# Moving the rounding of the last weight piece of each slot from GpSimd to ScalarE

## The chip, the cores and the metric

The kernel runs on one core of a Trainium2 chip. The metric is device time in microseconds, the median of several executions. An experiment on a changed kernel is compared with runs of the kernel before on the same chip.

## The reference

The reference is a two-layer decoder trunk over 256 tokens of width 1024. Each layer does RMSNorm, four mixer branches behind gates, cross-attention over 256 memory tokens, and a mixture of 16 experts. Only the last part matters here:

```
# hier_moe: top group, top 2 experts in it, weights `combine`
for e in range(16):
    he = silu(h @ w_gate[e]) * (h @ w_up[e])        # 1024 -> 512
    out = out + combine[..., e:e+1] * (he @ w_down[e])   # 512 -> 1024
```

All is float32. Each expert has three weight matrices of 2 MB (gate, up, down), and all 16 experts of both layers are loaded: 32 x 6 MB.

## The kernel before, in words

Before the expert stage of a layer runs the mixing, the cross-attention and the router; the change touches none of their instructions. In the expert stage the kernel goes through the 16 experts in order. One run through one expert is called a turn. The matrices land in three slots of the tile `ring`, one each for gate, up and down, and SyncE (SP) issues one load a slot as soon as the slot is free (L384 to L396).

TensorE multiplies in the float32r format, so each float32 weight is used as a sum of two float32r parts: `w_hi`, the rounded weight, and `w_lo`, the difference between the weight and `w_hi`. A slot is cut into four pieces of 128 x 1024, so an expert has twelve pieces, numbered n = 4j + i, where j = 0, 1, 2 is gate, up, down and i = 0 to 3 is the piece in the slot. `w_hi` and `w_lo` have six buffers (RP = 6): piece n may be written once TensorE has used piece n - 6, which the semaphore `w_used` tells.

For pieces i = 0, 1, 2 (`SHARED_PIECES`), ScalarE rounds (`pieces`, L1198, a Copy recorded at L994) and VectorE subtracts (`pieces`, L1858, recorded at L1863). For piece i = 3, GpSimd does both (`piece`, L1440: a cast at L1448, then a subtraction at L1451). The order of the work is written out by hand; every engine runs its own list in order and waits on semaphores. For one turn it is:

- TensorE (L910): gate product from pieces 0 to 3 ("widen 0"), transposed picks (L920), up product from pieces 4 to 7 ("widen 1"), then what fills the time until the activation is there: gathers for the next group of four experts (L871) and the scatter of the expert before (L885, L886), transposes of `hid` (L937), down product from pieces 8 to 11 (L948, L949).
- ScalarE (L1213): pieces 4, 5, 6, copy of the gate product (`gl`), `pickT`, piece 8, Silu, copy of the up product (`ul`), one gather copy (`ga`, not in the last four turns), pieces 9 and 10, copy of the transposed `hid` (`hidT`), pieces 0, 1, 2 of the next expert, two copies `y_hi`.
- VectorE (L1943): subtractions for 4, 5, 6, `gl` sum (L1947), subtraction for 8, `ul` sum (L1950), `hid` (L1954), subtraction for 9, gather copy `ga` (L1940), `hidT` low part (L1960), subtraction for 10, subtractions for 0, 1, 2 of the next expert, two `y_lo` (L1968).
- GpSimd (L1454): piece 7, copy of `pickT` to the upper partitions (L1460), piece 11, piece 3 of the next expert.

A slot is free for the next load when both VectorE's three subtractions (`w_lo`) and GpSimd's one (`w_lo_p`) from it are done.

Of the kernel before, what the change touches and what calls it, by code (L numbers as in the profile page):

```python
# [30 lines left out]
N_EXP = 16  # L31
# [39 lines left out]
def split_piece_used(n):  # L71
# [2 lines left out]

PER_TURN = dict(w_hi=9, w_lo=9, w_hi_p=3, w_lo_p=3, w_used=12, ga_mm=2, ga_ev_a=1, ga_ev_v=1,
                pickT_mm=1, pickT=1, pickT_p=1, gu_cp=2, gu_sum=2, act_gate=1, hid=1,
                hidT_mm=1, hidT_hi=1, hidT_lo=1, y_mm=1, y_hi=2, y_lo=2)
PER_PASS = dict(pick=1, sc_mm=4, x_acc=4)  # L80
# [2 lines left out]
RP = 6  # L83
# [5 lines left out]
SHARED_PIECES = (0, 1, 2)  # L89
# [7 lines left out]
def trunk(nc, T, out):  # L97
    with ExitStack() as ctx:  # L98
        def sb(name, shape, dt=F32):
            return ctx.enter_context(nc.sbuf_tensor(name, shape, dt))  # L100
# [3 lines left out]
        def sem(name):  # L104
            if name not in sems:
                sems[name] = ctx.enter_context(nc.semaphore(name))
            return sems[name]
# [154 lines left out]
        w_hi = sb("w_hi", [P, RP, PIECE], F32R)  # L262
        w_lo = sb("w_lo", [P, RP, PIECE], F32R)
# [40 lines left out]
        ld = [sem(f"loaded{s}") for s in range(NS)]  # L304
        slot_of = [i % NS for i in range(NCH)]
        e_slot = slot_of[ND:ND + 3]
        dense_loads = [slot_of[:ND].count(s) for s in range(NS)]
        loads = [n + PASSES * N_EXP for n in dense_loads]
# [27 lines left out]
        def turns_before(name, l, p, e):  # L336

            return (l * PASSES + p) * (N_EXP * PER_TURN[name]) + e * PER_TURN[name]

        def passes_before(name, l, p):  # L340

            return (l * PASSES + p) * PER_PASS[name]

        def skipped(name):

            return (PASSES - 1) * (N_EXP * PER_TURN[name] if name in PER_TURN else PER_PASS[name])

        def done_in_pass_0(name, l):

            return turns_before(name, l, 1, 0) if name in PER_TURN else passes_before(name, l, 1)  # L350

# [637 lines left out]
        def _(act):  # L989
            q = Order(act, "act")  # L990
            A = nc.scalar.activation

            def copy(dst, src, **kw):
                return A(dst, src, ACT.Copy, **kw)  # L994
# [37 lines left out]
            with act.Fori(0, L) as l:  # L1032
# [165 lines left out]
                def pieces(p, e, j, which):  # L1198

                    s_ = e_slot[j]  # L1200
                    act.wait_ge(ld[s_], l * (16 * loads[s_]) + 16 * (dense_loads[s_] + 1) + p * (16 * N_EXP) + e * 16)
                    for i in which:
                        n = 4 * j + i
                        act.wait_ge(sem("w_used"), turns_before("w_used", l, p, e) + n + 1)
                        copy(w_hi[:, n % RP, :], ring[:, s_, i * PIECE:i * PIECE + PIECE]).then_inc(sem("w_hi"), 1)

                def gathered(p, b, g, k):

                    act.wait_ge(sem("ga_mm"), turns_before("ga_mm", l, p, 0) + g * KD + k + 1)
                    copy(ga[:, g % 2, k].rearrange("p e a c -> p a e c"),  # L1210
                         bank[b][:].rearrange("p (a e c) -> p a e c", a=2, e=GROUP)).then_inc(sem("ga_ev_a"), 1)

                def turn(p, e):  # L1213
                    g, i = e // GROUP, e % GROUP
                    pieces(p, e, 1, SHARED_PIECES)

                    act.wait_ge(sem("w_used"), turns_before("w_used", l, p, e) + RP + 4)
                    copy(gl, bank[0][CAP:P, :]).then_inc(sem("gu_cp"), 1)
                    act.wait_ge(sem("pickT_mm"), turns_before("pickT_mm", l, p, e) + 1)
                    both = bank[2][0:CAP, 0:TB * IDC].rearrange("p (t n) -> p t n", t=TB)  # L1220
                    copy(pickT[0:CAP, e % 2, :].rearrange("p (t n) -> p t n", t=TB), both[:, :, 0:P])
                    copy(cw_parts[0:CAP], both[:, :, P + e:IDC:N_EXP], accum_out=cw[0:CAP, :]).then_inc(sem("pickT"), 1)
                    pieces(p, e, 2, (0,))
                    act.wait_ge(sem("gu_sum"), turns_before("gu_sum", l, p, e) + 1)
                    A(gl, gl, ACT.Silu).then_inc(sem("act_gate"), 1)

                    act.wait_ge(sem("w_used"), turns_before("w_used", l, p, e) + RP + 8)
                    copy(ul, bank[1][CAP:P, :]).then_inc(sem("gu_cp"), 1)
                    if g + 1 < GROUPS:
                        gathered(p, 0, g + 1, 2 * i)  # L1230
                    pieces(p, e, 2, (1, 2))
                    act.wait_ge(sem("hidT_mm"), turns_before("hidT_mm", l, p, e) + 1)
                    copy(hidT[:, :, 0, :], bank[1][:, 0:4 * CAP].rearrange("p (t c) -> p t c", t=4)).then_inc(sem("hidT_hi"), 1)
                    if e < N_EXP - 1:
                        pieces(p, e + 1, 0, SHARED_PIECES)
                    for nh in range(2):
                        if nh == 0:
                            act.wait_ge(sem("y_mm"), turns_before("y_mm", l, p, e) + 1)
                        else:

                            act.wait_ge(sem("w_used"), turns_before("w_used", l, p, e) + RP + 12)
                        copy(y_hi[:, nh * 512:nh * 512 + 512], bank[2 + nh][:]).then_inc(sem("y_hi"), 1)

                def one_pass(p):
                    if not isinstance(p, int):
                        pieces(p, 0, 0, SHARED_PIECES)
                    for k in range(0, KD, 2):
                        gathered(p, 4 + k % 4, 0, k)
                    for e in range(N_EXP):
                        turn(p, e)  # L1250

                pieces(0, 0, 0, SHARED_PIECES)
                for tb in range(TB):
                    act.wait_ge(sem("h_gained"), l * PER["h_gained"] + tb + 1)
                    copy(hs_hi[:, tb], h[:, tb, :].rearrange("p (f k) -> p k f", k=KD)).then_inc(sem("hs_hi"), 1)
# [1 line left out]
                A(rx[:, 2].rearrange("p a b -> p (a b)"), rx[:, 1].rearrange("p a b -> p (a b)"), ACT.Exp)  # L1257
                A(rx[:, 7].rearrange("p a b -> p (a b)"), rx[:, 6].rearrange("p a b -> p (a b)"), ACT.Exp).then_inc(sem("rt_x2"), 1)
                one_pass(0)

                act.wait_ge(sem("flag"), l + 1)
                more = q.more_passes()
                with act.If(more):
                    with act.Fori(1, PASSES) as p:
                        one_pass(p)
# [16 lines left out]
        def _(pool):  # L1282
            q = Order(pool, "pool")
            g = nc.gpsimd
# [63 lines left out]
            with pool.Fori(0, L) as l:  # L1348
# [66 lines left out]
                for n in range(16):  # L1415
                    i, tb, nh = n // 4, (n // 2) % 2, n % 2
                    pool.wait_ge(sem("mg_ev"), l * PER["mg_ev"] + n + 1)
                    q.settle()
                    src = gs[:, tb, i % 2, nh * 512:nh * 512 + 512]
# [20 lines left out]
                def piece(p, e, j):  # L1440
                    n = 4 * j + 3
                    s_ = e_slot[j]
                    pool.wait_ge(ld[s_], l * (16 * loads[s_]) + 16 * (dense_loads[s_] + 1) + p * (16 * N_EXP) + e * 16)
                    q.settle()
                    pool.wait_ge(sem("w_used"), turns_before("w_used", l, p, e) + n + 1)
                    q.settle()
                    src = ring[:, s_, 3 * PIECE:4 * PIECE]
                    g.tensor_copy(w_hi[:, n % RP, :], src).then_inc(sem("w_hi_p"), 1)  # L1448
                    pool.wait_ge(sem("w_hi_p"), turns_before("w_hi_p", l, p, e) + j + 1)
                    q.settle()  # L1450
                    g.tensor_tensor(w_lo[:, n % RP, :], src, w_hi[:, n % RP, :].bitcast(F32),  # L1451
                                    ALU.subtract).then_inc(sem("w_lo_p"), 1)

# [30 lines left out]
                        one_pass(p)  # L1484
                with pool.Else():

                    for name in ("w_hi_p", "pickT_p"):
                        pool.wait_ge(sem(name), done_in_pass_0(name, l))
                        pool.sem_inc(sem(name), skipped(name))
                    pool.wait_ge(sem("w_lo_p"), done_in_pass_0("w_lo_p", l) + LO_P_BIAS)  # L1490
                    pool.sem_inc(sem("w_lo_p"), skipped("w_lo_p"))
                q.leave()
# [7 lines left out]
        def _(dve):  # L1500
            q = Order(dve, "dve")
# [91 lines left out]
            with dve.Fori(0, L) as l:  # L1593
# [8 lines left out]
                s_ = lambda i: sp[:, i, :]  # L1602
# [65 lines left out]
                for n in range(8):  # L1668
# [4 lines left out]
                    for i in range(2):  # L1673
                        hd = n % 4 + 4 * i
                        src = rl[:, n % 2, i * wide:i * wide + wide]
# [30 lines left out]
                for u in range(3):  # L1706
                    dve.wait_ge(sem("dl_mm"), l * PER["dl_mm"] + u + 1)
                    n, wide = (4, P) if u == 0 else (2, S)
# [149 lines left out]
                def pieces(p, e, j, which):  # L1858

                    for i in which:  # L1860
                        n = 4 * j + i
                        dve.wait_ge(sem("w_hi"), turns_before("w_hi", l, p, e) + 3 * j + i + 1)
                        v.tensor_tensor(w_lo[:, n % RP, :], ring[:, e_slot[j], i * PIECE:i * PIECE + PIECE],  # L1863
                                        w_hi[:, n % RP, :].bitcast(F32), ALU.subtract).then_inc(sem("w_lo"), 1)

# [175 lines left out]
```

## Time and profile before

| what | value |
|---|---|
| median of 3 runs | 1618.54 us (1616.63 to 1620.39) |
| the profiled execution | 1624.06 us |
| its span | 1622.4 us |
| mean granted TensorE clock in it | 0.903 of full speed |
| busy: TensorE, VectorE, ScalarE, GpSimd | 1302.4, 977.4, 660.9, 753.3 us |

The profile is of one execution. A busy time is the union of an engine's instructions; an instruction that is held up after its start still counts as busy, so the duration of a single instruction is to be read beside the shortest of its kind. In the timeline, instructions of one kind that follow each other are merged into one line with their count ("x4") and the time from the first start to the last end. Times in brackets are idle time of the engine before the line, with what ended it.

### The profile page before, as it was taken

Reading aid. Unit: us, or ns where it says so; the run is one execution under the profiler, and the core shown is the slowest. Engines: PE = TensorE matmul, PEld = TensorE weight load, DVE = VectorE, ACT = ScalarE, POOL = GpSimd, SP = SyncE. Lnnn points to the kernel's source line nnn. Section 1 sums busy time; section 2 is a strip of 40 time slices with the busy share of each in tenths; the row PEclk is TensorE's granted clock in tenths of the full one; section 3 lists DMA queues with packets and bytes.
Section 4 is the critical chain, followed back from the end, with each engine's and each line's share of the span. In section 5 each row is a group of like instructions: output and inputs, shape, how many; then the busy total and the mean of one; then the engine's idle time right before and its main releaser. Section 6 shows DMA issues by size and latency. Waiting matters only on the chain. (4 is left out here: it accounts for less than half of the span.)

```text
span 1622.4 us, 18087 instructions
## 1 busy us (share of the span) xinstructions
PE 1302.4 (80%) x5124; PEld 934.1 (58%) x5124; DVE 977.4 (60%) x1261; ACT 660.9 (41%) x1005; POOL 753.3 (46%) x625
## 2 busy tenths in 40 slices
PE   4999978999487877787769998898975777777773
PEld 2874644676365655565548645466854565556552
DVE  3306365422679888888622254654127888898885
ACT  4122303322365655555430412043234655556552
POOL 5730063200656666776436202612007666766663
PEclk8999989999589999998879998999996889999987
DMA  8443213432557777878264431164144777877771
GB/s 218 132 156 104 104 52 120 152 143 104 124 209 267 275 292 272 302 281 292 103 203 131 156 105 52 52 217 146 52 169 70 266 273 290 298 278 281 289 287 60
DMA packets 58384, 299.25 MB, mean 184 GB/s; under 512 B 4016, under 2 KB 8224, under 8 KB 45728
## 3 DMA queue, kind: packets, MB, share of 16 engines
q1 hardware_dynamic: 55536, 294.07, 50.9%
q0 software_dynamic: 2736, 3.87, 2.2%
q8 instruction: 48, 0.79, 0.2%
q14 instruction: 64, 0.52, 0.1%
HBM read 296.88 MB, written 1.05 MB: 184 GB/s over the span
## 5 line engine op out<-in xcount | busy, mean ns | idle before, releaser
L1863 DVE TENSOR_TENSOR w_lo<-ring,w_hi 128x1024 fp32r<-128x1024 f32 x288 | 482.4, 1718 | 8.8 <-ACT w_hi L994 6.8
L994 ACT ACTIVATE w_hi<-ring 128x1024 fp32r<-128x1024 f32 x328 | 330.0, 1054 | 40.7 <-PE bank L533 26.4
L906 PE MATMUL bank<-w_hi,ga 128*128 128x512 f32 x512 | 226.1, 442 | 101.3 <-DVE w_lo L1863 83.9
L1448 POOL CAST w_hi<-ring 128x1024 fp32r<-128x1024 f32 x96 | 181.6, 1892 | 204.4 <-PE bank L949 170.9
L1451 POOL TENSOR_TENSOR w_lo<-ring,w_hi 128x1024 fp32r<-128x1024 f32 x96 | 267.7, 2789 | 17.9 <-POOL w_hi L1448 17.9
L468 PE MATMUL bank<-ring,hT 128*128 128x512 f32 (+2 forms) x576 | 217.9, 539 | 4.0 <-ACT hT L1029 2.2
L907 PE MATMUL bank<-w_lo,ga 128*128 128x512 f32 x512 | 215.3, 420 | 0.0
L906 PEld LDWEIGHTS bank<-w_hi,ga 128*128 128x128 f32 x512 | 104.4, 204 | 155.2 <-DVE w_lo L1863 109.9
L468 PEld LDWEIGHTS bank<-ring,hT 128*128 128x128 f32 x576 | 113.5, 199 | 102.0 <-issue 96.7
L948 PE MATMUL bank<-w_hi,hidT 128*128 128x512 f32 x256 | 120.1, 469 | 41.7 <-DVE hidT L1960 41.7
L462 PE MATMUL bank<-hT,ring 128*128 128x256 f32 (+1 forms) x544 | 119.3, 380 | 1.9 <-DVE hT L1569 1.9
L949 PE MATMUL bank<-w_lo,hidT 128*128 128x512 f32 x256 | 116.4, 455 | 0.0
L907 PEld LDWEIGHTS bank<-w_lo,ga 128*128 128x128 f32 x512 | 105.4, 206 | 19.0
L462 PEld LDWEIGHTS bank<-hT,ring 128*128 128x128 f32 (+1 forms) x544 | 99.9, 184 | 20.7 <-DVE hT L1569 2.3
L948 PEld LDWEIGHTS bank<-w_hi,hidT 128*128 128x128 f32 x256 | 58.2, 227 | 59.1 <-issue 37.9
L1408 POOL TENSOR_TENSOR gk<-dl,E 128x512 f32<-128x512 f32 x8 | 10.1, 1267 | 170.8 <-DVE dl L1777 170.8
L1804 DVE TENSOR_TENSOR w_lo<-ring,w_hi 128x1024 fp32r<-128x1024 f32 x40 | 49.4, 1275 | 63.8 <-ACT w_hi L994 63.8
L1426 POOL TENSOR_TENSOR h<-h,gs 128x512 f32<-128x512 f32 x24 | 33.8, 1433 | 104.3 <-DVE gs L1785 104.3
L1287 POOL DMA_DIRECT2D gul<-in_norm_ffn x2 | 1.3, 635 | 172.2 <-DVE x L1851 172.2
L994 ACT ACTIVATE gul<-bank 64x512 f32<-64x512 f32 x64 | 38.1, 595 | 82.8 <-PE bank L907 82.7
L531 PE MATMUL bank<-w_hi,hT_hi 128*128 128x512 f32 x160 | 64.6, 404 | 3.9 <-DVE hT_lo L1821 3.9
L1072 ACT ACTIVATE gs<-bank 128x512 f32<-128x512 f32 x32 | 19.1, 597 | 116.6 <-PE bank L468 93.9
(441 smaller groups left out, 2151.9 us busy)
## 6 DMA issues: line engine op xcount, KB each, us to landing
ring<-in_w_e_gate SPq DMA_DIRECT2D x32, 2048.0 KB, 8.1
ring<-in_w_e_up SPq DMA_DIRECT2D x32, 2048.0 KB, 8.2
ring<-in_w_e_down SPq DMA_DIRECT2D x32, 2048.0 KB, 8.1
ring<-in_w_in SPq DMA_DIRECT2D x24, 2048.0 KB, 8.3
ring<-in_w_ckv SPq DMA_DIRECT2D x4, 2048.0 KB, 9.6
ring<-in_w_branch SPq DMA_DIRECT2D x4, 2048.0 KB, 10.3
ring<-in_w_out SPq DMA_DIRECT2D x4, 2048.0 KB, 11.2
ring<-in_w_cq SPq DMA_DIRECT2D x2, 2048.0 KB, 14.7
```

What stands on the lines that cost most here:

```text
L462: ins = mm(dst, w[:, k, c0:c0 + m], src[:, k, :], start=(k == 0), stop=(k == KD - 1))
L468: ins = mm(dst, src[:, k, tb * P:tb * P + P], w[:, k, c0:c1], start=(k == 0), stop=(k == KD - 1))
L531: mm(bank[b0 + tb][:], t_hi, w_hi[:, n % RP, c], start=(k == 0), stop=False)
L906: mm(bank[j][:], tile, w_hi[:, n % RP, c], start=(k == 0), stop=False)
L907: ins = mm(bank[j][:], tile, w_lo[:, n % RP, c], start=False, stop=(k == KD - 1))
L948: mm(bank[2 + nh][:], tile, w_hi[:, n % RP, c], start=(t == 0), stop=False)
L949: ins = mm(bank[2 + nh][:], tile, w_lo[:, n % RP, c], start=False, stop=(t == 3))
L994: return A(dst, src, ACT.Copy, **kw)
L1448: g.tensor_copy(w_hi[:, n % RP, :], src).then_inc(sem("w_hi_p"), 1)
L1451: g.tensor_tensor(w_lo[:, n % RP, :], src, w_hi[:, n % RP, :].bitcast(F32), ALU.subtract).then_inc(sem("w_lo_p"), 1)
L1804: v.tensor_tensor(w_lo[:, n % RP, :], ring[:, s_, i * PIECE:i * PIECE + PIECE], w_hi[:, n % RP, :].bitcast(F32), ALU.subtract).then_inc(se ...
L1863: v.tensor_tensor(w_lo[:, n % RP, :], ring[:, e_slot[j], i * PIECE:i * PIECE + PIECE], w_hi[:, n % RP, :].bitcast(F32), ALU.subtract).then ...
```

## The change

ScalarE rounds all four pieces of every slot, GpSimd only subtracts for piece 3, and it waits for ScalarE's semaphore `w_hi` in place of its own waits for the load and for `w_used`. ScalarE's copies go at the end of each group of pieces: piece 7 before the `gl` copy, piece 11 before the `hidT` copy, piece 3 of the next expert before the `y_hi` copies, and in the router stage piece 3 of the first expert before the copies of `h`. The counts of `w_hi` follow.

```diff
-PER_TURN = dict(w_hi=9, w_lo=9, w_hi_p=3, w_lo_p=3, w_used=12, ga_mm=2, ga_ev_a=1, ga_ev_v=1,
+PER_TURN = dict(w_hi=12, w_lo=9, w_lo_p=3, w_used=12, ga_mm=2, ga_ev_a=1, ga_ev_v=1,
@@ ScalarE, turn
-                    pieces(p, e, 1, SHARED_PIECES)
+                    pieces(p, e, 1, range(4))
@@
-                    pieces(p, e, 2, (1, 2))
+                    pieces(p, e, 2, (1, 2, 3))
                     act.wait_ge(sem("hidT_mm"), turns_before("hidT_mm", l, p, e) + 1)
                     copy(hidT[:, :, 0, :], ...).then_inc(sem("hidT_hi"), 1)
                     if e < N_EXP - 1:
-                        pieces(p, e + 1, 0, SHARED_PIECES)
+                        pieces(p, e + 1, 0, range(4))
@@ ScalarE, router stage
-                pieces(0, 0, 0, SHARED_PIECES)
+                pieces(0, 0, 0, range(4))
@@ GpSimd, piece
-                    pool.wait_ge(ld[s_], l * (16 * loads[s_]) + 16 * (dense_loads[s_] + 1) + p * (16 * N_EXP) + e * 16)
-                    q.settle()
-                    pool.wait_ge(sem("w_used"), turns_before("w_used", l, p, e) + n + 1)
+                    pool.wait_ge(sem("w_hi"), turns_before("w_hi", l, p, e) + n + 1)
                     q.settle()
                     src = ring[:, s_, 3 * PIECE:4 * PIECE]
-                    g.tensor_copy(w_hi[:, n % RP, :], src).then_inc(sem("w_hi_p"), 1)
-                    pool.wait_ge(sem("w_hi_p"), turns_before("w_hi_p", l, p, e) + j + 1)
-                    q.settle()
                     g.tensor_tensor(w_lo[:, n % RP, :], src, w_hi[:, n % RP, :].bitcast(F32),
                                     ALU.subtract).then_inc(sem("w_lo_p"), 1)
@@ VectorE, pieces
-                        dve.wait_ge(sem("w_hi"), turns_before("w_hi", l, p, e) + 3 * j + i + 1)
+                        dve.wait_ge(sem("w_hi"), turns_before("w_hi", l, p, e) + n + 1)
```

## Rows read from the trace of the kernel before

**Rows 1.** The page: busy time of each engine; a load's median time to landing.

```profile
PE 1302.4 (80%) x5124; PEld 934.1 (58%) x5124; DVE 977.4 (60%) x1261; ACT 660.9 (41%) x1005; POOL 753.3 (46%) x625
...
ring<-in_w_e_down SPq DMA_DIRECT2D x32, 2048.0 KB, 8.1
```

**Rows 2.** The `ul` sums of the first expert stage: durations, first and last start.

```profile
L1950 DVE TENSOR_TENSOR gul<-bank,gul x16: 682/683/684, 459.8 to 795.4; 64x512 f32<-64x512 f32 x16
```

**Rows 3.** Windows: length; busy PE, PEld, DVE, ACT, POOL (instructions); granted clock, DMA share, GB/s.

```profile
459.80:795.40 335.60, 259.03 (x1017) 197.41 (x1018) 290.20 (x238) 193.72 (x283) 228.13 (x107) 0.90 0.76 275
...
592.90:594.90 2.00, 2.00 (x9) 1.65 (x10) 1.67 (x2) 0.63 (x1) 1.52 (x2) 1.00 0.96 270
...
615.10:618.80 3.70, 3.67 (x10) 2.96 (x11) 1.70 (x2) 0.63 (x1) 3.04 (x3) 0.54 0.88 275
```

**Rows 4.** Waits in 459.8 to 795.4: total us, times, longest.

```profile
POOL w_hi L1448 <- PE bank L949: 86.0, 15, 6.5
PEld bank L906 <- DVE w_lo L1863: 55.0, 30, 2.6
```

**Rows 5.** Timeline of VectorE, from one `ul` sum to the second one after it.

```profile
575.11 0.68 DVE L1950 TENSOR_TENSOR gul<-bank,gul 64x512 f32<-64x512 f32 x1 [2.65 <-ACT gul L994]
...
576.68 1.23 DVE L1863 TENSOR_TENSOR w_lo<-ring,w_hi 128x1024 fp32r<-128x1024 f32 x1
...
578.43 0.41 DVE L1960 TENSOR_TENSOR hidT<-bank,hidT 128x256 fp32r<-128x256 f32 x1
578.76 5.46 DVE L1863 TENSOR_TENSOR w_lo<-ring,w_hi 128x1024 fp32r<-128x1024 f32 x4
584.15 1.27 DVE L1968 TENSOR_TENSOR y_lo<-bank,y_hi 128x512 fp32r<-128x512 f32 x2
585.35 7.50 DVE L1863 TENSOR_TENSOR w_lo<-ring,w_hi 128x1024 fp32r<-128x1024 f32 x3
592.77 0.68 DVE L1947 TENSOR_TENSOR gul<-bank,gul 64x512 f32<-64x512 f32 x1
...
595.68 0.68 DVE L1950 TENSOR_TENSOR gul<-bank,gul 64x512 f32<-64x512 f32 x1 [1.11 <-ACT gul L994]
596.55 2.05 DVE L1954 SCALAR_TENSOR_TENSOR gul<-gul,cw 64x512 f32<-64x512 f32 x1 [0.19 <-DVE gul L1950]
...
615.00 0.67 DVE L1947 TENSOR_TENSOR gul<-bank,gul 64x512 f32<-64x512 f32 x1
...
619.47 0.68 DVE L1950 TENSOR_TENSOR gul<-bank,gul 64x512 f32<-64x512 f32 x1 [2.67 <-ACT gul L994]
```

**Rows 6.** Timeline of VectorE, single subtractions out of the merged lines.

```profile
582.16 2.06 DVE L1863 TENSOR_TENSOR w_lo<-ring,w_hi 128x1024 fp32r<-128x1024 f32 x1
...
589.46 3.39 DVE L1863 TENSOR_TENSOR w_lo<-ring,w_hi 128x1024 fp32r<-128x1024 f32 x1
```

**Rows 7.** Timeline of GpSimd in the same turn.

```profile
581.25 1.89 POOL L1448 CAST w_hi<-ring 128x1024 fp32r<-128x1024 f32 x1 [5.33 <-PE bank L949]
583.32 3.15 POOL L1451 TENSOR_TENSOR w_lo<-ring,w_hi 128x1024 fp32r<-128x1024 f32 x1 [0.18 <-POOL w_hi L1448]
...
588.63 3.13 POOL L1451 TENSOR_TENSOR w_lo<-ring,w_hi 128x1024 fp32r<-128x1024 f32 x1 [0.18 <-POOL w_hi L1448]
...
595.66 2.40 POOL L1451 TENSOR_TENSOR w_lo<-ring,w_hi 128x1024 fp32r<-128x1024 f32 x1 [0.18 <-POOL w_hi L1448]
```

**Rows 8.** Timeline of ScalarE in the same turn.

```profile
575.60 1.99 ACT L994 ACTIVATE w_hi<-ring 128x1024 fp32r<-128x1024 f32 x2
577.89 0.38 ACT L994 ACTIVATE hidT<-bank 128x256 fp32r<-128x256 f32 x1 [0.30 <-PE bank L937]
...
582.48 1.09 ACT L994 ACTIVATE y_hi<-bank 128x512 fp32r<-128x512 f32 x2 [1.22 <-PE bank L949]
...
588.80 1.05 ACT L994 ACTIVATE w_hi<-ring 128x1024 fp32r<-128x1024 f32 x1
```

**Rows 9.** Timeline of SyncE: the load of the next `down` matrix.

```profile
580.26 0.33 SPq L396 DMA_DIRECT2D ring<-in_w_e_down  x1
```

More of the change, by code:

```diff
@@ L1245, in one_pass @@
                     if not isinstance(p, int):
-                        pieces(p, 0, 0, SHARED_PIECES)
+                        pieces(p, 0, 0, range(4))
                     for k in range(0, KD, 2):
@@ L1485, in _ @@
                 with pool.Else():
-                    for name in ("w_hi_p", "pickT_p"):
-                        pool.wait_ge(sem(name), done_in_pass_0(name, l))
-                        pool.sem_inc(sem(name), skipped(name))
+                    pool.wait_ge(sem("pickT_p"), done_in_pass_0("pickT_p", l))
+                    pool.sem_inc(sem("pickT_p"), skipped("pickT_p"))
                     pool.wait_ge(sem("w_lo_p"), done_in_pass_0("w_lo_p", l) + LO_P_BIAS)
```

## The prediction, made before the changed kernel was run

> **What bounds the kernel now.** I read the busy times first. TensorE is busy for 80% of the span and VectorE for 60% [rows 1], but the change touches only the two expert stages. The window over the first of them, from the first `ul` sum at 459.8 us to the last at 795.4 [rows 2], says more: 15 turns in 335.6 us, 22.37 us a turn, VectorE busy for 290.2 of it (86%), TensorE 259.0, GpSimd 228.1, ScalarE 193.7, DMA share 0.76 [rows 3]. The waits come next: TensorE waits 30 times for VectorE's `w_lo`, 55.0 us in total, while GpSimd sits idle for 86.0 us before its cast of piece 3, waiting for TensorE to use piece 9 [rows 4]. So the loop is closed by VectorE, and GpSimd has time to spare.
>
> Then the timeline of VectorE over two turns [rows 5]. Their periods, from `ul` sum to `ul` sum, are 595.68 - 575.11 = 20.57 and 619.47 - 595.68 = 23.79 us; I call them short and long. I read this pair as the steady pattern; it makes 44.36 us, 22.18 a turn. In the short turn VectorE has no idle time of note from `hidT` at 578.43 to the `gl` sum at 592.77, so each microsecond lost in that stretch moves the turn. Behind the `gl` sum lie TensorE's last two up pieces, the `ul` copy and the `ul` sum: 2.91 us in the short turn and 4.47 in the other. The difference is the clock: 1.00, the 2.4 GHz level, in 592.9 to 594.9, but 0.54, most of it at 1.2 GHz, in 615.1 to 618.8 [rows 3]; in the second case TensorE had just stood still for want of the same `w_lo`. The mean tail is 3.69.
>
> **What holds VectorE.** A subtraction alone takes 1.23 us at 576.68 [rows 5]. The one at 582.16 takes 2.06 and the one at 589.46 takes 3.39 [rows 6]. Beside GpSimd's rows this has one reading. The cast runs 581.25 to 583.14; the subtraction started at 582.16 ends 1.08 us after the cast does. GpSimd's subtraction issued at 588.63 ends at 591.76; the VectorE one issued at 589.46 ends at 592.85, again 1.09 later [rows 6, 7]. GpSimd's own takes 2.40 when nothing is in its way (595.66) and 3.15 when it is issued inside a VectorE subtraction [rows 7]. So a VectorE operation on two SBUF tensors and a GpSimd subtraction exclude each other, and a GpSimd one that is waiting goes before VectorE's next. A full hit costs VectorE 3.39 - 1.23 = 2.16 us, a cast 2.06 - 1.23 = 0.83. `y_lo`, with one operand in PSUM, runs 1.27 for two beside GpSimd's 3.15 and pays nothing [rows 5, 7]. `hid` does pay: 2.05 us at 596.55 under the subtraction of 595.66 [rows 5, 7].
>
> The page "SBUF — State Buffer" of the Trainium skill (section on the two separate sides) says in my words that whoever starts first holds the shared ports for its whole instruction and the other is fully blocked. The trace agrees for the subtractions and not for the cast: the cast of 581.25 started while VectorE was inside a subtraction, and neither was lengthened. What the rule as stated would make of the sum is the third rival.
>
> **The change, part by part (short turn, zero at the `ul` sum, 575.11).**
>
> 1. Removed: three casts a turn on GpSimd. Two of them hit VectorE. The line of three (585.35, 7.50 us) is 3 x 1.13 us of issue distance (5.46 for four, less one 0.83 hit, gives 1.13 to 1.16) plus 4.0 of blocking: 2.16 for the full subtraction, 0.83 for a cast, and about 1.0 for the tail of the subtraction of 583.32, which runs to 586.47 [rows 5 to 7]. The line of four contains the other 0.83. The third cast lies in VectorE's idle time. Gain: 2 x 0.83 = 1.7 us. Bounds: 0, if something else ends those waits, and 2 x 1.89, a cast's whole duration.
>
> 2. Added: three ScalarE copies of 1.0 us (1.99 for two [rows 8]).
>  - Piece 7: ScalarE's idle 1.2 us before `y_hi`, and VectorE's lateness in the up pieces, cover it. The `gl` copy after it is not wanted before the `gl` sum. Cost 0, and 1.0 without that cover.
>  - Piece 11, before `hidT`: ScalarE ended its two copies at 577.59 and was idle for 0.30 until TensorE's transposes were there [rows 8]. The third copy ends at about 578.6, so `hidT`, the `hidT` low part and the start of the down product come 0.7 us later. Cost 0.7 (bounds 0 and 1.0). In the last four turns ScalarE has no `ga` copy ahead, and I take 0.2.
>  - Piece 3 of the next expert needs piece 9 used, 581.25 before. ScalarE has 1.22 us idle before `y_hi` [rows 8], and the copy fits. Cost 0 (bound 1.0).
>
> 3. Moved: the GpSimd subtractions, and this decides.
>  - Piece 11. Before, the subtraction ran at 573.54, in VectorE's wait for `ul`, or at 595.66, where it held `hid`. Now it starts when ScalarE's third copy ends: 1.99 + 0.49 + 1.0 + 0.18 (the handover on GpSimd [rows 7]) = +3.65, and runs to +6.05. VectorE issues the subtraction for piece 10 at 578.76 + 0.7, +4.35, and is held to +6.05, so it ends at +7.1 in place of +5.55. Cost 1.55; bounds 0 (it falls in idle time) and 2.16.
>  - Piece 3 of the next expert. ScalarE's copy ends at about +7.75 and GpSimd asks at +7.9, in the middle of VectorE's four. Before it was at +8.2 but met the two `y_lo`, so only 1.0 was lost. Now `y_lo` is 2.2 us further away, and the hit is full: 2.16 - 1.0 = 1.15. Bounds -1.0 and 1.15.
>  - Piece 7. Its copy is the fourth after `y_hi` and waits for piece 1 to be used; GpSimd asks near the end of `y_lo` and hits one of the three up subtractions, as before. Cost 0; bounds -2.16 and 0.
>
> 4. Semaphores. The wait for `w_used` and for the load leave GpSimd; ScalarE makes both before it rounds, so nothing is queued behind them that was not. A GpSimd wait now holds `pickT_p` behind piece 7; TensorE's scatter wants that only after the next up product. 0.
>
> 5. Loads. The `down` slot is freed at +7.1 and not at 580.26, +5.15 [rows 9]. With 8.1 us to landing [rows 1] it is there at +15.2. ScalarE rounds piece 8 at 588.80, +13.7 before and over 15 after, ahead of a Silu that waits for the `gl` sum. Hidden; without that cover up to 1.5. The other two have more room.
>
> The sum for a turn with gathers: 0.7 - 1.7 + 1.55 + 1.15 = +1.7 us at the `gl` sum, which stood at 592.77 - 575.11 = +17.66 and goes to about +19.4. In the long turn the `gl` sum stood at 615.00 - 595.68 = +19.32: it had paid a held `hid` (1.3) and a slow down product. Both of these vanish in VectorE's backlog afterwards: `hid` meets no subtraction any more, and `y_hi`, at +8.8 with the fast clock and at most +11 with the slow one, is ready before VectorE ends its four at +12.7. So after the change every turn is like the long one up to the `gl` sum: 19.4. I leave the tail as it is, 3.69 on average. Then a turn is 23.1 against 22.18: +0.92.
>
> Thirty turn intervals make 27.6. The measured mean, 22.37, exceeds the pair's 22.18 by 0.19, which is 5.7 us over 30: those other turns are slower already, and I take half of it as absorbing part of the cost, -2.8. The last turn of each stage also holds a delayed down product, 0.5 each, +1. In the router stage GpSimd loses a cast ahead of its subtraction, but VectorE's queue there is held by what follows it as well: 0, within 2 a layer. Sum +26. The profiled execution, 1624.06 us (span 1622.4), would become 1650; it stood 5.5 us above the median, so the median goes from 1618.5 to about 1645.
>
> **Rivals.**
> - Faster. The two cast hits vanish and the subtractions cost no more than today. One mechanism: which VectorE operation a GpSimd subtraction meets. For: GpSimd becomes idle by 5.7 us a turn, and VectorE is the bound. Against: subtraction 11 starts at +3.65 and the low part of `hidT` at +4.0, so the VectorE burst is right behind it. It decides if that subtraction and that of piece 3 still meet `ul`, `ga` or `y_lo`. Price: 1.7 in the short turn, 0.83 in the long one, 1.27 x 30 = 38: 1580; with ScalarE's 0.7 in 24 turns charged, 1597.
> - Only ScalarE's delay counts: 0.7 x 24 = 17: 1636. For: VectorE's blocking might merely change places. Against: the sum above.
> - The exclusive hold as the page states it. Each cast hit is then worth 1.89, not 0.83, and point 1 gains 2.1 more a short turn: 0.92 - 1.05 on average, so about 1615, no change. Against: the 2.06 row [rows 6].
> - The clock. TensorE stands still for longer after the change. If every tail ran at 1.2 GHz (4.47 in place of 3.69), 0.78 x 30 = 23 more: 1668. If every tail were fast, 1622.
>
> **How the numbers follow.** My forecast, with the subtraction hits and a mixed clock (1636 to 1655), has 0.50; only ScalarE's delay or fast tails (1622 to 1636) 0.12; slow tails (1655 to 1672) 0.12; no change 0.08; faster 0.18. A measurement of this kernel tells 0.2%, 3.2 us, from no change. So slower 0.74, same 0.08, faster 0.18. Range 1604 to 1666: it leaves out most of the faster case and the end of the slow-clock case. The likeliest case's own range is 1622 to 1666.
>
> **What would show it.** In the trace after: `hidT` on ScalarE right behind a line of three roundings, with no idle time; GpSimd's subtraction about 3.6 us after the `ul` sum; in VectorE's line after `hidT` two held subtractions, so that four take over 8 us and not 5.46; the `gl` sum at 19.4 in nearly every turn, the alternation of 20.6 and 23.8 gone; no 2.06 us durations left. It is wrong if VectorE's durations of over 3 us are no more frequent than one or two a turn, if `y_lo` waits for `y_hi`, or if turns come out under 22.

## The result: slower by 2.1%, and where the time went

The changed kernel takes 1651.7 us (median of 4 runs, 1648.71 to 1656.16) against 1618.06 us for the kernel before (4 runs). The ratio is 1.0209, 95% interval 1.0182 to 1.0236. The forecast was 1645, and slower. The interval leaves no doubt that it is slower; whether by more or by less than 2% it does not settle. The profiled execution has a span of 1649.2 us, 26.8 more than the 1622.4 before. The profiled execution of the kernel before took 1624.06 us, 3.7 more than the longest of its four timed runs, while that of the changed kernel, 1650.97 us, lies at the median; so the spans differ by less than the medians.

First the page of the changed kernel, busy times and the largest group (line, engine, operation, shapes, count, then busy us and mean ns, then idle time before and what ended it):

```profile
PE 1316.2 (80%) x5124; PEld 925.2 (56%) x5124; DVE 1008.1 (61%) x1261; ACT 750.7 (46%) x1101; POOL 571.7 (35%) x529
...
L1857 DVE TENSOR_TENSOR w_lo<-ring,w_hi 128x1024 fp32r<-128x1024 f32 x288 | 536.0, 1903 | 8.7 <-ACT w_hi L994 7.9
```

GpSimd is busy for 181.6 us less than in [rows 1], and VectorE for 30.7 us more with the same 1261 instructions. Its added time is time in which its instructions are held up after their start. The numbers of three lines move: L1857 is L1863 of before, L1944 the `ul` sum L1950, L1941 the `gl` sum L1947, and GpSimd's subtraction is L1446.

The first expert stage, from the first `ul` sum to the last, by a window (length; busy PE, PEld, VectorE, ScalarE, GpSimd; granted clock, DMA share, GB/s), and the longest waits in it:

```profile
457.20:809.10 351.90, 272.41 (x1018) 196.98 (x1019) 308.01 (x238) 235.89 (x328) 140.38 (x60) 0.89 0.71 262
```

```profile
POOL w_lo L1446 <- ACT w_hi L994: 202.5, 45, 9.0
PEld bank L906 <- DVE w_lo L1857: 70.6, 64, 2.6
```

15 turns take 351.9 us, where [rows 3] had 335.6: 23.46 us a turn and not 22.37. GpSimd waits for ScalarE for 202.5 us, and the wait of TensorE's weight loads (PEld) for `w_lo` has grown from 55.0 [rows 4] to 70.6 us. So GpSimd was relieved and the engine that closes the loop was not.

One turn of VectorE, to be laid beside [rows 5]:

```profile
573.35 0.68 DVE L1944 TENSOR_TENSOR gul<-bank,gul 64x512 f32<-64x512 f32 x1 [2.52 <-ACT gul L994]
...
577.09 0.42 DVE L1954 TENSOR_TENSOR hidT<-bank,hidT 128x256 fp32r<-128x256 f32 x1 [0.34 <-ACT hidT L994]
577.43 8.62 DVE L1857 TENSOR_TENSOR w_lo<-ring,w_hi 128x1024 fp32r<-128x1024 f32 x4
585.97 1.28 DVE L1962 TENSOR_TENSOR y_lo<-bank,y_hi 128x512 fp32r<-128x512 f32 x2
587.16 5.86 DVE L1857 TENSOR_TENSOR w_lo<-ring,w_hi 128x1024 fp32r<-128x1024 f32 x3
592.95 0.67 DVE L1941 TENSOR_TENSOR gul<-bank,gul 64x512 f32<-64x512 f32 x1
...
597.25 0.68 DVE L1944 TENSOR_TENSOR gul<-bank,gul 64x512 f32<-64x512 f32 x1 [2.50 <-ACT gul L994]
```

The four subtractions after `hidT` take 8.62 us, before 5.46; the three up ones take 5.86, before 7.50. The `gl` sum stands at 592.95 - 573.35 = +19.60 us and the next `ul` sum at +23.90. Nearly every turn with gathers looks like this to three tenths, in both stages: the `gl` sum stands at +19.6 to +19.8, the next `ul` sum 4.1 to 4.4 us behind it, and the alternation of 20.57 and 23.79 is gone. Single subtractions out of these lines, and GpSimd's three, show the holds:

```profile
577.43 3.00 DVE L1857 TENSOR_TENSOR w_lo<-ring,w_hi 128x1024 fp32r<-128x1024 f32 x1
...
582.62 3.42 DVE L1857 TENSOR_TENSOR w_lo<-ring,w_hi 128x1024 fp32r<-128x1024 f32 x1
...
588.30 3.39 DVE L1857 TENSOR_TENSOR w_lo<-ring,w_hi 128x1024 fp32r<-128x1024 f32 x1
```

```profile
576.96 2.39 POOL L1446 TENSOR_TENSOR w_lo<-ring,w_hi 128x1024 fp32r<-128x1024 f32 x1 [8.93 <-ACT w_hi L994]
581.48 3.48 POOL L1446 TENSOR_TENSOR w_lo<-ring,w_hi 128x1024 fp32r<-128x1024 f32 x1 [2.13 <-ACT w_hi L994]
588.14 2.47 POOL L1446 TENSOR_TENSOR w_lo<-ring,w_hi 128x1024 fp32r<-128x1024 f32 x1 [3.18 <-ACT w_hi L994]
```

Each GpSimd subtraction now falls into a row of VectorE subtractions and costs it 1.8 to 2.2 us; the durations of 2.06 us, the cast hits of [rows 6], are gone. ScalarE shows why the first comes so late and with it `hidT`; there is no idle time before `hidT` now, where [rows 8] had 0.30:

```profile
573.84 2.94 ACT L994 ACTIVATE w_hi<-ring 128x1024 fp32r<-128x1024 f32 x3
576.68 0.37 ACT L994 ACTIVATE hidT<-bank 128x256 fp32r<-128x256 f32 x1
```

**The account.** I add up, turn by turn, the time from a `ul` sum to the `gl` sum and from there to the next `ul` sum (the tail), 30 turns in both stages. The first grows by 10.3 + 12.6 = 22.9 us, the tail by 6.0 + 5.7 = 11.7 us, together 34.6. Outside this, 7.7 us are won: 1.9 before anything that differs (at the start of the program), the rest in the router stages and behind the last `ul` sums. 34.6 - 7.7 is the 26.8 us of the spans, to rounding. Inside these sums, the first turn of each stage became shorter, 20.25 us and not 24.26. Why is not shown: with the same list of work on GpSimd, warm5_after below has 22.5 us there.

### The profile page after: what moved, and what is told of

It reads as the page before. It is cut to its first block and busy times, and to the rows that moved or that the text cites. A ratio compares the mean times of both kernels' runs of the same rounds, so it can differ in the third digit from the quotient of the medians.

```text
span 1649.2 us, 17857 instructions
## 1 busy us (share of the span) xinstructions
PE 1316.2 (80%) x5124; PEld 925.2 (56%) x5124; DVE 1008.1 (61%) x1261; ACT 750.7 (46%) x1101; POOL 571.7 (35%) x529
## 5 line engine op out<-in xcount | busy, mean ns | idle before, releaser
L1857 DVE TENSOR_TENSOR w_lo<-ring,w_hi 128x1024 fp32r<-128x1024 f32 x288 | 536.0, 1903 | 8.7 <-ACT w_hi L994 7.9
L994 ACT ACTIVATE w_hi<-ring 128x1024 fp32r<-128x1024 f32 x424 | 422.5, 1053 | 33.6 <-PE bank L533 24.8
L1446 POOL TENSOR_TENSOR w_lo<-ring,w_hi 128x1024 fp32r<-128x1024 f32 x96 | 266.5, 2776 | 445.9 <-ACT w_hi L994 445.9
L906 PE MATMUL bank<-w_hi,ga 128*128 128x512 f32 x512 | 237.1, 463 | 102.6 <-DVE w_lo L1857 93.9
L907 PE MATMUL bank<-w_lo,ga 128*128 128x512 f32 x512 | 222.2, 434 | 0.0
L907 PEld LDWEIGHTS bank<-w_lo,ga 128*128 128x128 f32 x512 | 109.3, 213 | 19.8
L949 PE MATMUL bank<-w_lo,hidT 128*128 128x512 f32 x256 | 110.6, 432 | 0.0
L948 PEld LDWEIGHTS bank<-w_hi,hidT 128*128 128x128 f32 x256 | 53.5, 209 | 93.5 <-issue 51.6
L1798 DVE TENSOR_TENSOR w_lo<-ring,w_hi 128x1024 fp32r<-128x1024 f32 x40 | 49.4, 1275 | 62.1 <-ACT w_hi L994 62.1
L1944 DVE TENSOR_TENSOR gul<-bank,gul 64x512 f32<-64x512 f32 x32 | 21.8, 682 | 70.3 <-ACT gul L994 70.3
L532 PE MATMUL bank<-w_lo,hT_hi 128*128 128x512 f32 x160 | 62.9, 393 | 0.0
## 6 DMA issues: line engine op xcount, KB each, us to landing
ring<-in_w_branch SPq DMA_DIRECT2D x4, 2048.0 KB, 10.3
```

Of the source, the lines that this page charges most:

```text
L532: mm(bank[b0 + tb][:], t_hi, w_lo[:, n % RP, c], start=False, stop=False)
L906: mm(bank[j][:], tile, w_hi[:, n % RP, c], start=(k == 0), stop=False)
L907: ins = mm(bank[j][:], tile, w_lo[:, n % RP, c], start=False, stop=(k == KD - 1))
L948: mm(bank[2 + nh][:], tile, w_hi[:, n % RP, c], start=(t == 0), stop=False)
L949: ins = mm(bank[2 + nh][:], tile, w_lo[:, n % RP, c], start=False, stop=(t == 3))
L1798: v.tensor_tensor(w_lo[:, n % RP, :], ring[:, s_, i * PIECE:i * PIECE + PIECE], w_hi[:, n % RP, :].bitcast(F32), ALU.subtract).then_inc(se ...
```

## The experiments

All ratios are to runs of the kernel before on the same chip. Theory A says that what counts is the place of each GpSimd operation in VectorE's line; B, that ScalarE's added work is the cost; C, TensorE's clock. "Turn by turn" means the two sums of the account above, each over 30 turns of the profiled execution. Line numbers differ from run to run; tile names and shapes tell what an instruction is.

### One slot at a time

ScalarE rounds the last piece of one slot only, and GpSimd keeps its cast for the other two:

```diff
-                    pieces(p, e, 1, SHARED_PIECES)          # up_only
+                    pieces(p, e, 1, range(4))
-                        pieces(p, e + 1, 0, SHARED_PIECES)  # gate_only
+                        pieces(p, e + 1, 0, range(4))
-                    pieces(p, e, 2, (1, 2))                 # down_only
+                    pieces(p, e, 2, (1, 2, 3))
```

> Of the change, only the up slot is done: ScalarE rounds piece 7, GpSimd keeps its casts of pieces 3 and 11. Theory A (exclusive hold between GpSimd and VectorE's two-input operations, and where each GpSimd operation falls): one cast hit of 0.83 us a turn goes and no subtraction moves into a worse place, so 0.8 x 30 = 24 us faster than before, about 1594. Theory B (the extra ScalarE work on the path is what costs): ScalarE has 1.2 us idle there, so within 3 us of before or slower. Theory C (only TensorE's clock): no ordered change.

Measured: 1590.25 us, ratio 0.983 (0.981 to 0.9849).

> Only the gate slot is done: ScalarE rounds piece 3 of the next expert. Theory A: the cast hit inside VectorE's line of four goes (0.83 in the short turn), the subtraction still meets y_lo and then one subtraction, 0.6 to 0.85 us a turn, so 18 to 25 us faster, about 1597. Theory B: same or slower, since the copy stands ahead of y_hi.

Measured: 1593.24 us, ratio 0.985 (0.982 to 0.988).

> Only the down slot is done: ScalarE rounds piece 11 before the hidT copy. Theory A: the whole loss sits here. hidT 0.4 us later, GpSimd's subtraction at +3.6 us holds the subtraction for piece 10 (1.8 us), y_lo moves away so that the subtraction of piece 3 hits in full (1.2 more) while a cast hit may go (0.8 less): the gl sum at about +20.2, turns of 24.3 us, 60 us slower than before, about 1678, so slower than the full change. Theory B: 0.4 us in 24 turns, about 10 us slower, 1628.

Measured: 1664.78 us, ratio 1.0295 (1.0276 to 1.0315).

The mean duration of a VectorE subtraction in the window 457 to 800 us goes the same way. One row each from up_only, gate_only and down_only (1706 ns before and 1896 ns after the whole change, in their first stage):

```profile
L1870 DVE TENSOR_TENSOR w_lo<-ring,w_hi 128x1024 fp32r<-128x1024 f32 x137 | 214.8, 1610 | 6.6 <-ACT w_hi L997 5.1
```

```profile
L1870 DVE TENSOR_TENSOR w_lo<-ring,w_hi 128x1024 fp32r<-128x1024 f32 x137 | 219.7, 1647 | 1.1 <-ACT w_hi L997 0.6
```

```profile
L1870 DVE TENSOR_TENSOR w_lo<-ring,w_hi 128x1024 fp32r<-128x1024 f32 x129 | 253.1, 2004 | 0.4 <-ACT w_hi L997 0.2
```

Two thirds of the change are each a gain of 1.5 to 1.7%, and the down slot alone loses 3%. The loss is less than the 60 us that were expected; the `gl` sum stands at about +20.5 there, but the tail is 3.53 us on average. The sum of the parts, -28 - 25 + 46 = -7 us, is not the whole, +34. Turn by turn, up_only and gate_only shorten the stretch up to the `gl` sum by 33 us each; on top of the down slot the two together shorten it by 31. The tails grow by 4 and 13 us in the single ones, and by 19 when both are put on top of the down slot. So what the casts of pieces 3 and 7 cost depends on where the rest stands, and a part of what is won before the `gl` sum is paid back in the tail. B does not explain two gains from added ScalarE work.

### ScalarE made slower, all else as before

```diff
-                        copy(w_hi[:, n % RP, :], ring[...]).then_inc(sem("w_hi"), 1)
+                        if i == 2:   # eight copies of 128 columns, the last one signals
+                            ...
```

> The kernel before, with ScalarE alone made slower: its rounding of the third piece of each slot is done in eight parts of 128 columns, which adds about 1 us where the change adds a whole rounding. GpSimd keeps its casts and subtractions. Theory A (place of the GpSimd holds): only the part before hidT is felt, 0.4 to 0.7 us in the 24 turns with gathers, so 0 to 17 us slower than before, 1618 to 1636. Theory B (ScalarE's added work makes the loss): 30 us or more slower, 1650.

Measured: 1619.5 us, ratio 1.0007 (0.9997 to 1.0017). The eight parts added less than meant: two roundings take 2.64 us, 0.65 more than in [rows 8], and the low part of `hidT` comes at 578.74 - 575.31 = +3.43, only 0.11 later than before.

```profile
575.80 2.64 ACT L994 ACTIVATE w_hi<-ring 128x1024 fp32r<-128x1024 f32 x9
578.35 0.36 ACT L994 ACTIVATE hidT<-bank 128x256 fp32r<-128x256 f32 x1
```

It shows that 0.65 us more of ScalarE work in each slot costs nothing that can be measured; for the full rounding ahead of `hidT` it is too weak a test.

### Piece 11 rounded behind hidT

```diff
-                    pieces(p, e, 2, (1, 2, 3))
+                    pieces(p, e, 2, (1, 2))
                     ...
                     copy(hidT[:, :, 0, :], ...).then_inc(sem("hidT_hi"), 1)
+                    pieces(p, e, 2, (3,))
```

> The changed kernel with ScalarE's rounding of piece 11 put behind the hidT copy. Theory A: hidT comes 0.4 us earlier, but GpSimd then asks inside VectorE's subtraction for piece 10 and the next one is held in full (2.2 in place of 1.8): the gl sum stays at +19.6 within 0.2, 1652 within 6. Theory B (ScalarE's delay of hidT): 0.4 to 0.7 us in 24 turns back, 10 to 17 us faster than the change, 1635 to 1642.

Measured: 1626.35 us, ratio 1.0053 (1.0036 to 1.007). That is 25 us faster than the change and outside both expectations, nearer to B's number than to A's. The trace shows that B's reason is not the one:

```profile
594.58 0.68 DVE L1945 TENSOR_TENSOR gul<-bank,gul 64x512 f32<-64x512 f32 x1 [1.10 <-ACT gul L994]
...
598.23 1.22 DVE L1858 TENSOR_TENSOR w_lo<-ring,w_hi 128x1024 fp32r<-128x1024 f32 x1
599.67 7.58 DVE L1858 TENSOR_TENSOR w_lo<-ring,w_hi 128x1024 fp32r<-128x1024 f32 x3 [0.23 <-ACT w_hi L994]
...
614.17 0.67 DVE L1942 TENSOR_TENSOR gul<-bank,gul 64x512 f32<-64x512 f32 x1
...
617.07 0.68 DVE L1945 TENSOR_TENSOR gul<-bank,gul 64x512 f32<-64x512 f32 x1 [1.10 <-ACT gul L994]
```

The low part of `hidT` is 0.43 us earlier and the subtraction for piece 10 runs freely, but the next ones are held in its place, and the `gl` sum is at 614.17 - 594.58 = +19.59, as A said, not a tenth better. What fell is the tail: 2.90 us for 4.30; turn by turn the tails are 30.6 us shorter and the stretches up to the `gl` sum 4.4 us longer. The stretch of the tail ran at full clock, that of the changed kernel (591.75 to 594.90) at 0.66:

```profile
614.20:616.40 2.20, 2.10 (x10) 1.77 (x11) 1.77 (x3) 0.63 (x1) 0.00 (x0) 1.00 0.78 164
```

```profile
591.75:594.90 3.15, 3.08 (x8) 2.16 (x9) 3.00 (x3) 0.63 (x1) 0.19 (x1) 0.66 0.89 281
```

The slow stretch is not gone, it lies earlier, behind another wait of TensorE: the granted clock is 0.55 from 607.2 to 611.0. There it does not delay the `gl` sum. Why it moved was not tested.

### TensorE kept busy in its idle time

Matmuls that serve nothing, into PSUM bank 3, which is free there:

```diff
+                def idle_work(p, e, count):
+                    if e > 0:
+                        pe.wait_ge(sem("y_lo"), turns_before("y_lo", l, p, e - 1) + 2)
+                    for _ in range(count):
+                        mm(bank[3][:, 0:256], hs_hi[:, 0, 0, :], pick[:, 0, 0:GROUP, :]..., start=True, stop=True)
@@ widen, ahead of each piece
+                        if n == 6:
+                            idle_work(p, e, 16)
@@ behind the transposes of hid
+                    idle_work(p, e, 10)
```

> The changed kernel with matmuls that serve nothing put into two idle times of TensorE: 16 of 256 columns ahead of piece 6, 10 behind the transposes of hid, into a PSUM bank that is free then. If the tail from the gl sum to the ul sum (4.3 us after, 2.9 with the fast clock) is long because TensorE has stood still before it, the tail falls to about 2.9 to 3.2 us and the time by 1.1 to 1.4 us in 30 turns, 33 to 42 us, to about 1613; the gl sum stays at +19.6. If the clock does not depend on that, the time is that of the change, 1652, or a little more.

Measured: 1679.14 us, ratio 1.0373 (1.0355 to 1.039), 27 us slower than the change. The clock did stay up (1.00 over the turn from 650.74 to 674.74), but I had put the work on the path. TensorE's timeline: piece 5 could start only at 669.14, and the sixteen matmuls then stood for 2.06 us ahead of piece 6, which was ready at about the time they began.

```profile
669.94 0.40 PE L917 MATMUL bank<-w_lo,ga 128*128 128x512 f32 x1
670.17 2.06 PE L903 MATMUL bank<-pick,hT_hi 128*128 128x256 f32 x16
672.07 0.40 PE L916 MATMUL bank<-w_hi,ga 128*128 128x512 f32 x1
```

With 14 of them ahead of piece 5 instead, in TensorE's wait itself, and 10 behind the transposes as in warm_after:

> The changed kernel with the same idle matmuls, but 14 of them ahead of piece 5, where TensorE waits 2.1 us for a held subtraction (in the run before they stood ahead of piece 6 and took 2.0 us on the path), and 10 behind the transposes. Theory: the clock stays at 2.4 GHz, the tail is 2.9 us and not 4.3, the gl sum stays at +19.6: 22.5 us a turn and 1.4 x 27 = 38 us faster than the change, 1612 to 1620. If the clock is not what makes the tail long: 1652 as the change.

Measured: 1624.81 us, ratio 1.0033 (1.0019 to 1.0047), 27 us faster than the change and 5 above the expected range. The window of the first stage shows a full clock, and the sums of one turn a tail of 618.32 - 615.41 = 2.91 us with the `gl` sum at +19.64:

```profile
457.20:800.00 342.80, 294.09 (x1408) 224.16 (x1407) 314.40 (x241) 240.72 (x334) 141.53 (x62) 1.00 0.73 270
```

```profile
595.77 0.68 DVE L1955 TENSOR_TENSOR gul<-bank,gul 64x512 f32<-64x512 f32 x1 [1.10 <-ACT gul L1005]
...
615.41 0.67 DVE L1952 TENSOR_TENSOR gul<-bank,gul 64x512 f32<-64x512 f32 x1
...
618.32 0.68 DVE L1955 TENSOR_TENSOR gul<-bank,gul 64x512 f32<-64x512 f32 x1 [1.10 <-ACT gul L1005]
```

Turn by turn the tails are 37.6 us shorter than in the changed kernel. The stretches up to the `gl` sum are 6.7 us longer, which comes from the first turn of each stage (19.6 us for 16.0), and 5.5 us more lie outside the turns; why is open. So most of the loss of 34 us depends on the clock in the tail. Does the same help the kernel before (14 ahead of piece 6, where that kernel waits, and 6 behind the transposes)?

> The kernel before with idle matmuls: 14 of 256 columns ahead of piece 6, where TensorE waits 2.1 us, and 6 behind the transposes. It tells what the clock alone costs before the change. In the long turn the slow clock costs 1.6 us in the tail and up to 1.8 in the down product; but after a fast tail GpSimd's subtraction for piece 11 meets hid (1.3 us), which a slow tail avoids. With a fast clock in every turn I expect turns of 21.4 to 22.2 us, 0 to 25 us faster than before, about 1605. Then the holds alone make the changed kernel with warm TensorE (1625) some 20 us slower. If it is at 1570 or less (every turn 20.6), the holds make 50 us and the clock took most of the gap away; if it is 1618, the clock costs the kernel before nothing.

Measured: 1617.08 us, ratio 0.9997 (0.9988 to 1.0007). No. A turn of it:

```profile
636.68 0.68 DVE L1961 TENSOR_TENSOR gul<-bank,gul 64x512 f32<-64x512 f32 x1 [1.11 <-ACT gul L1005]
637.55 2.06 DVE L1965 SCALAR_TENSOR_TENSOR gul<-gul,cw 64x512 f32<-64x512 f32 x1 [0.19 <-DVE gul L1961]
...
656.00 0.67 DVE L1958 TENSOR_TENSOR gul<-bank,gul 64x512 f32<-64x512 f32 x1
...
658.91 0.68 DVE L1961 TENSOR_TENSOR gul<-bank,gul 64x512 f32<-64x512 f32 x1 [1.10 <-ACT gul L1005]
```

The tails are all fast, 2.91 us, but now every turn is a long one up to the `gl` sum (+19.32), because GpSimd's subtraction for piece 11 meets `hid` each time (2.06 us). A turn of 22.25 us is the mean of the old pair. With TensorE kept busy in both kernels, the change costs 1624.8 - 1617.1 = 8 us; the other 26 come with the clock, as far as the idle matmuls, which stand at different places in the two, do nothing else. In the kernel before, a slow tail paid for itself, in the changed one it does not.

### No GpSimd subtraction at all

All twelve subtractions go to VectorE, which gives it 3 x 1.14 us more work a turn:

```diff
-                    pieces(p, e, 1, SHARED_PIECES)      # VectorE, likewise gate and down
+                    pieces(p, e, 1, range(4))
-                    piece(p, e, 1)                      # GpSimd, likewise the other two
```

> The change with GpSimd's subtraction taken away too: VectorE subtracts all twelve pieces. It adds 3 x 1.13 us of work to the engine that closes the loop and takes away three holds of 1.8, 2.2 and 2.2 us. Theory A: the gl sum comes at 19.6 - 6.2 + 3.4 = +16.8 us, turns of 19 to 20.5 us, 50 to 95 us faster than the changed kernel, 1560 to 1600, if loads keep up. Theory B (ScalarE): no better than the change, 1652, as ScalarE does the same. Plain work count on VectorE: 3.4 us a turn slower, 1750.

Measured: 1507.38 us, ratio 0.9317 (0.9296 to 0.9338): 144 us faster than the change and 111 faster than the kernel before. That is also 53 us below the lower end of what was expected. The engine with the longest line was given more to do and the turn fell from 23.9 to 18.62 us:

```profile
549.38 0.68 DVE L1913 TENSOR_TENSOR gul<-bank,gul 64x512 f32<-64x512 f32 x1 [0.19 <-ACT gul L984]
...
553.46 6.89 DVE L1826 TENSOR_TENSOR w_lo<-ring,w_hi 128x1024 fp32r<-128x1024 f32 x6
...
561.46 4.62 DVE L1826 TENSOR_TENSOR w_lo<-ring,w_hi 128x1024 fp32r<-128x1024 f32 x4
566.00 0.68 DVE L1910 TENSOR_TENSOR gul<-bank,gul 64x512 f32<-64x512 f32 x1
...
568.00 0.68 DVE L1913 TENSOR_TENSOR gul<-bank,gul 64x512 f32<-64x512 f32 x1 [0.19 <-ACT gul L984]
```

The `gl` sum is at +16.62 (expected +16.8). I had left the tail out of the gain: it is 2.00 us and not 2.9, since the `gl` sum now stands behind the subtraction for piece 7, so that one piece less is left for TensorE behind it. Turn by turn, 82.6 us are won up to the `gl` sum, where the holds were, and 65.0 us in the tails, where the shorter tail and the clock come together; this run does not separate those two. VectorE is busy for 96% of this stretch (159.81 of 166.60 us), with 341 GB/s of loads:

```profile
549.40:716.00 166.60, 147.82 (x614) 110.77 (x613) 159.81 (x169) 141.78 (x197) 18.97 (x9) 0.95 0.91 341
```

With the rounding of piece 11 put behind `hidT` as well:

> All twelve subtractions on VectorE, and ScalarE's rounding of piece 11 behind the hidT copy. With no GpSimd hold left, the 0.4 us of ScalarE before hidT should show undiluted: 0.4 x 24 = 10 us faster than the version with the rounding first, about 1497. If VectorE's own work fills the turn, less: 1507.

Measured: 1496.0 us, ratio 0.924 (0.9224 to 0.9255), 11 us faster than the version above. The low part of `hidT` comes at 552.00 - 548.69 = +3.31 and not +3.73, and with no hold left these 0.42 us of ScalarE show undiluted:

```profile
552.00 0.42 DVE L1924 TENSOR_TENSOR hidT<-bank,hidT 128x256 fp32r<-128x256 f32 x1
```

This is the best version found, 7.6% faster than the kernel before.

Last, GpSimd gets one subtraction back, for piece 7:

> As the version with all twelve subtractions on VectorE (1507), but GpSimd subtracts piece 7. The price of one hold by itself. Theory A: VectorE saves 1.13 us of its own and pays 2.16, 1.05 us a turn, 31 us in 30 turns: 1538. If GpSimd's help were help, 1.13 us a turn less: 1473.

Measured: 1535.95 us, ratio 0.9489 (0.9471 to 0.9507), 29 us slower than with none. The number is the expected one, the way there is not. The three up subtractions of VectorE run freely (3.49 us), and it is GpSimd's that is held, for 2.6 us of its 4.96:

```profile
568.64 3.49 DVE L1852 TENSOR_TENSOR w_lo<-ring,w_hi 128x1024 fp32r<-128x1024 f32 x3
572.04 0.67 DVE L1936 TENSOR_TENSOR gul<-bank,gul 64x512 f32<-64x512 f32 x1
572.64 2.80 DVE L1852 TENSOR_TENSOR w_lo<-ring,w_hi 128x1024 fp32r<-128x1024 f32 x1
```

```profile
569.40 4.96 POOL L1447 TENSOR_TENSOR w_lo<-ring,w_hi 128x1024 fp32r<-128x1024 f32 x1 [13.42 <-ACT w_hi L995]
```

It gets its turn only when the third has ended, and TensorE waits for piece 7 until 574.36. The turn has its `gl` sum at +15.5 us and a tail of 4.2, where the version with none has +16.6 and 2.0. Whoever is held, the piece costs more than the 1.14 us it saves.

## Why the prediction was right, and where it was not

- What bounds: right. VectorE's line closes the loop; without holds on it the stretch up to the `gl` sum fell from 19.6 to 16.62 us, with 3.4 us of work added (all_vector).
- Point 1, the casts: the price of 0.83 us a hit is right, the reading behind it is wrong. I took 1.89 us for a cast's own time and wrote that a cast started under a running subtraction lengthened neither and that the exclusive hold does not cover it. But a cast alone takes 1.04 us, as at 459.71, where VectorE has only the `ul` sum with its operand in PSUM, and in down_only at 568.69, beside `y_lo`:

```profile
459.71 1.04 POOL L1448 CAST w_hi<-ring 128x1024 fp32r<-128x1024 f32 x1 [0.49 <-POOL pickT L1460]
```

```profile
568.69 1.04 POOL L1455 CAST w_hi<-ring 128x1024 fp32r<-128x1024 f32 x1 [2.51 <-PE bank L910]
```

  The cast of 581.25 started under this subtraction, waited for its end at 582.25 and ended 0.89 us later; then the next VectorE subtraction, issued at 582.16, had its turn:

```profile
581.03 1.22 DVE L1863 TENSOR_TENSOR w_lo<-ring,w_hi 128x1024 fp32r<-128x1024 f32 x1
```

  Of the 94 casts from 457 us on in the kernel before, 2 take 1.04 us, and the other 92 end 0.89 to 0.91 us behind the end of a VectorE operation with two SBUF operands. So the exclusive hold is there for the cast as well, and with it a full hit costs 0.83 us. The third rival, which priced a hit at 1.89, had the right rule and the wrong price, and was no rival. Alone, the two slots bring 28 and 25 us, together 53, more than the 38 that the first rival allowed for all casts. A cast taken out also moves the subtraction behind it; how much of the rest that explains is not shown.
- Point 2, `hidT` later: 0.42 us measured (VectorE's low part at +3.74 against +3.32), 0.7 written. The time until GpSimd's subtraction, +3.61 for +3.65, was right. That the copies of pieces 3 and 7 cost nothing, as written, fits the gains of up_only and gate_only.
- Point 3, the moved subtractions: right in place and price. The durations of 3.00, 3.42 and 3.39 us are 1.77, 2.19 and 2.16 us of holding over 1.23; forecast were 1.55, 2.16 and 2.16. The `gl` sum was forecast at +19.4 in nearly every turn and stands at +19.6; the end of VectorE's four at +12.7 and at +12.7.
- The tail: wrong. I took the mean of one pair of turns, 3.69, and left it. Over all 30 turns it was 3.78 before and is 4.16 after (4.30 in the turn shown), which makes 11.7 us where I had written 0. The rival on the clock had 4.47, and warm5_after shows that it is the clock.
- Outside the turns: I wrote 0 for the router and +1 for the stage ends; they gave back 5.8 us, and 1.9 us more came before anything that differs. For the turns up to the `gl` sum I had 24.8 us after the absorbed part; they made 22.9: the first turns made 9.4 us less than before, and the other 28 made 1.15 us more each, where I had 0.92.
- The sum: in the profiled span +26 was forecast and +26.8 measured. That is partly luck, since 11.7 us of tail that I had not written met 7.7 us of gain that I had not written either. The median came out 6.7 us above 1645 in the last step, where I carried the 5.5 us between profiled execution and median over to the changed kernel: the profiled execution was forecast at 1650 and took 1650.97 us, which is 0.7 under the median and not 5.5 above it.
- The rule that a waiting GpSimd operation goes before VectorE's next one holds most of the time, not always. In the kernel before, 2 of the 94 casts waited for a further subtraction, this one up to 493.33; in vector_gp7 the subtraction waited for two further ones. What decides it stays open.

```profile
491.20 3.05 POOL L1448 CAST w_hi<-ring 128x1024 fp32r<-128x1024 f32 x1 [5.02 <-PE bank L949]
```

- What I did not see: that the kernel before has a second long way of 19.3 us which a fast clock brings out in every turn (warm_before), so that the holds alone, with TensorE kept busy in both, cost 8 us and not 26.

## What to carry to other kernels

Where two engines exclude each other, work given to the second is not free: its price is what it holds up on the first. Here a subtraction of 1.14 us on VectorE cost VectorE 2.2 us when GpSimd did it. Before relieving an engine that is not the bound, follow where its remaining operations will fall; one change made in three places can be two gains and one larger loss, so time the places apart. Read a duration beside the shortest of its kind before you call it the operation's own time: the cast's 1.89 us were 1.04 and a wait. And read the matmul rate behind every wait of TensorE: behind waits of the same 2.1 us the clock was full in one turn and low in the next.

## What the runs showed of the hardware

- A GpSimd subtraction of 128 x 1024 float32 from SBUF takes 2.39 us alone and a GpSimd cast of that size 1.04 us. Each excludes VectorE operations with two SBUF operands. A VectorE subtraction held by them takes 3.39 and 2.06 us in place of 1.23.
- A GpSimd operation that starts under such a VectorE operation waits for its end: the cast then ends 0.9 us behind it and the subtraction 2.2 to 2.3. The wait counts as busy time in the profile of both engines, so a cast shows 1.89 or 2.04 us.
- VectorE operations with one operand in PSUM are not held: `y_lo` takes 1.27 us for two beside a running GpSimd subtraction [rows 5, 7].
- A waiting GpSimd operation mostly went as soon as the VectorE operation in progress ended (90 of the 92 casts that waited in the kernel before; subtractions of 3.49 us at most before and after). VectorE passed it with one more subtraction in the other two casts (3.05 us) and with two in vector_gp7 (4.96 us).
- The granted clock of the stretch behind TensorE's wait of 2.1 us was 1.00 in one turn and 0.54 in the next before the change [rows 3], 0.66 after it, and 1.00 with 14 idle matmuls in that wait. A fast clock was worth 27 us to the changed kernel and nothing to the kernel before.
